# All sums of weight blocks on VectorE: 20 blocks in the first block's output projection, 12 in the third feed-forward

## The chip, the cores and the metric

The kernel runs on one core of one Trainium2 chip, as one program of 53741 instructions in the profile. The time is device microseconds (us) of that core from start to end. Engines are named as in the profile: PE is TensorE (matmuls; PEld its weight loads), DVE is VectorE, ACT is ScalarE, POOL is GpSimd, SP is SyncE, which here only issues DMA transfers.

## The reference

Three transformer-like blocks run one behind the other on a sequence of 1024 tokens of width 1024, all in float32. Cut to what the change touches:

```python
def first_block(x, ...):
    ...
    y = jnp.einsum('bse,ed->bsd', mixed, w_out)      # mixed: 2048 wide, w_out: 2048 x 1024
    ...

def third_block(x, ..., w1, b1, w2, b2, ...):
    ...
    ff = jnp.square(jax.nn.relu(jnp.einsum('btd,df->btf', x, w1[l]) + b1[l]))   # 1024 -> 4096
    ff = jnp.einsum('btf,fd->btd', ff, w2[l]) + b2[l]                           # 4096 -> 1024
    x = layer_norm(DEEPNORM_ALPHA * x + ff, ln2_g[l], ln2_b[l])
```

## The kernel before

**Precision.** A float32 product is made of three products of a faster format: every operand is split into a high part (ACT copies it into the format) and a low part (DVE subtracts the high part from the original), and PE adds high x high, high x low and low x high.

**The third feed-forward** multiplies by a scheme with seven products in place of eight (Strassen-like). It cuts weights in quarters, and four of its seven products take sums of quarters, called S1 to S4, as weights. A *block of sums* is a tile of 128 x 4 x 512 numbers: four quarters q11, q12, q21, q22 come in from the weights in HBM in two transfers of 512 KB, four additions or subtractions of 128 x 512 turn them in place into S4, S3, S1 and S2, and two transfers of 512 KB store them to HBM, from where the feed-forward later loads them like other weights. There are 32 such blocks, 16 for each of the two matrices. The class `WeightSums` (line 1659) does this work: `loads` and `stores` are SP's part, `sums` (line 1699) the arithmetic, each a generator that yields the planned time of its next instruction. Each of the four operations waits for the one before it (semaphore `made`), and the first two also for a transfer (`landed`).

**Where the blocks are made.** `SumsAhead` (line 1725) makes the first 8 blocks and the 16 of the second matrix, 24 in all, far ahead of their use: during the output projection of the first block, in two tiles in turn. The other 8 are made inside the third feed-forward by the object `late` (line 5090), in one tile that lies in a part of y not yet used. In both places the arithmetic is POOL's.

**The output projection** of the first block is `project_chain` (line 307). It has 16 steps, here also called blocks of the projection and counted from 0: two stages of eight output tiles each, of 128 x 1024 results. For each, SP loads 512 KB of weights, ACT makes their high part (line 477), DVE their low part (line 538), PE runs 48 matmuls (lines 429 to 431 for the first two, then 446 to 448), and the result is copied by ACT in the first stage (line 650) or added by DVE in the second (line 655). Two tiles in turn hold the weights, two the results. At its start ACT and DVE also split the inputs: eight tiles mixg, then eight tiles mixa (lines 284 and 291). The loops of PE, ACT and DVE are hardware loops (`Fori`).

**What sets the order.** Each engine has a program of its own, in fixed order, and waits at semaphores. `weave` (line 666) merges generators into one such order by their planned times; the times order instructions on one engine and make nothing wait. The whole phase ends when all engines are through, and SP's program there ends with a wait for all stores of sums (line 372).

**The third feed-forward's engines.** DVE adds products out of the eight banks of results (`combining`, line 5295 by its helper), subtracts what is kept of them (`subtracting`, line 5347, which waits for stores SP issues), makes the low parts of weights (`SevenWeights.low`, line 1816) in seven slots, and those of the inputs. SP's one queue carries raw weights (line 1802), stores of products and differences (lines 5176 and 5183) and the loads and stores of sums (1679, 1686).

## Time and profile before

| | us |
|---|---|
| median of 3 runs | 3939.45 (3936.46 to 3943.36) |
| the profiled execution | 3941.63 |
| its span | 3940.0 |
| PE busy | 3699.2 |
| DVE busy | 2198.1 |
| ACT busy | 1611.7 |
| POOL busy | 822.8 |

The profile is of one execution. Busy time is the sum over an engine's instructions; those of different engines lie beside each other. "Idle before, releaser" is the time an engine stood still ahead of an instruction, and what ended it. TensorE's granted clock is a share of 2.4 GHz. Times in a timeline count from the start of the span.

### The profile page before, as it was taken

Reading aid. Unit: us, or ns where it says so; the run is one execution under the profiler, and the core shown is the slowest. Engines: PE = TensorE matmul, PEld = TensorE weight load, DVE = VectorE, ACT = ScalarE, POOL = GpSimd, SP = SyncE. Lnnn points to the kernel's source line nnn. Section 1 sums busy time; section 2 is a strip of 40 time slices with the busy share of each in tenths; the row PEclk is TensorE's granted clock in tenths of the full one; section 3 lists DMA queues with packets and bytes.
Section 4 is the critical chain, followed back from the end, with each engine's and each line's share of the span. In section 5 each row is a group of like instructions: output and inputs, shape, how many; then the busy total and the mean of one; then the engine's idle time right before and its main releaser. Section 6 shows DMA issues by size and latency. Waiting matters only on the chain. (4 is left out here: it accounts for less than half of the span.)

```text
span 3940.0 us, 53741 instructions
## 1 busy us (share of the span) xinstructions
PE 3699.2 (94%) x20308; PEld 2898.6 (74%) x20308; DVE 2198.1 (56%) x3779; ACT 1611.7 (41%) x2993; POOL 822.8 (21%) x581
## 2 busy tenths in 40 slices
PE   9998999898998887999999989999979988999998
PEld 5787888685766775888888857777667766778876
DVE  3343332415365757766663353666666658667777
ACT  4365222313355514433331154555533326456443
POOL 1000000574002314322210040111433322210012
PEclk9999999998999999999999999999989999999999
DMA  2111111683111112232242021111121105977662
GB/s 88 32 33 47 40 43 43 231 312 123 44 49 49 62 38 97 70 104 94 93 166 86 32 52 55 51 51 49 54 82 50 52 23 180 312 248 249 210 203 95
DMA packets 187744, 393.25 MB, mean 100 GB/s; under 512 B 27992, under 2 KB 34072, under 8 KB 187496
## 3 DMA queue, kind: packets, MB, share of 16 engines
q1 hardware_dynamic: 187496, 389.93, 30.0%
q8 instruction: 157, 2.57, 0.3%
q14 instruction: 91, 0.75, 0.1%
HBM read 293.85 MB, written 97.98 MB: 99 GB/s over the span
## 5 line engine op out<-in xcount | busy, mean ns | idle before, releaser
L1894 PE MATMUL b_ffn_space<-b_ffn_in_hi,b_ffn_wh 128*128 128x512 f32 x896 | 352.1, 393 | 8.2 <-DVE b_ffn_wl L1816 7.2
L1896 PE MATMUL b_ffn_space<-b_ffn_in_hi,b_ffn_wl 128*128 128x512 f32 x896 | 349.9, 390 | 0.0
L1594 PE MATMUL b_ffn_space<-b_ffn_in_hi,b_ffn_wh 128*128 128x512 f32 x728 | 283.9, 390 | 3.3 <-DVE b_ffn_in_x_low L1454 3.3
L1596 PE MATMUL b_ffn_space<-b_ffn_in_hi,b_ffn_wl 128*128 128x512 f32 x728 | 282.8, 389 | 0.0
L1350 ACT ACTIVATE b_ffn_wh<-b_ffn_raw 128x512 fp32r<-128x512 f32 (+1 forms) x152 | 93.6, 619 | 296.8 <-PE b_ffn_space L1622 166.0
L1894 PEld LDWEIGHTS b_ffn_space<-b_ffn_in_hi,b_ffn_wh 128*128 128x128 f32 x896 | 168.7, 188 | 51.7 <-issue 12.9
L1895 PE MATMUL b_ffn_space<-b_ffn_in_x_low,b_ffn_wh 128*128 128x512 f32 x512 | 202.2, 395 | 0.0
L1896 PEld LDWEIGHTS b_ffn_space<-b_ffn_in_hi,b_ffn_wl 128*128 128x128 f32 x896 | 168.7, 188 | 36.4
L1356 DVE TENSOR_TENSOR b_ffn_wl<-b_ffn_raw,b_ffn_wh 128x512 fp32r<-128x512 f32 (+1 forms) x152 | 118.2, 778 | 118.1 <-ACT b_ffn_wh L1350 116.4
L1705 POOL TENSOR_TENSOR b_out_block<-b_out_block 128x512 f32<-128x512 f32 x24 | 37.6, 1565 | 669.6 <-DMA b_out_block<-w 669.6
L1816 DVE TENSOR_TENSOR b_ffn_wl<-b_ffn_raw,b_ffn_wh 128x512 fp32r<-128x512 f32 x224 | 168.5, 753 | 15.1 <-ACT b_ffn_wh L1810 14.3
L762 PE MATMUL na_feed_acc<-b3v_x_hi,na_feed_wh 128*128 128x512 f32 x384 | 164.4, 428 | 2.4 <-DVE na_feed_wl L745 2.4
L1595 PE MATMUL b_ffn_space<-b_ffn_in_x_low,b_ffn_wh 128*128 128x512 f32 x416 | 164.3, 395 | 0.0
L1594 PEld LDWEIGHTS b_ffn_space<-b_ffn_in_hi,b_ffn_wh 128*128 128x128 f32 x728 | 136.3, 187 | 37.3 <-DVE b_ffn_in_x_low L1454 4.1
L1810 ACT ACTIVATE b_ffn_wh<-b_ffn_raw 128x512 fp32r<-128x512 f32 x224 | 133.1, 622 | 64.4 <-PE b_ffn_space L1896 64.3
L1596 PEld LDWEIGHTS b_ffn_space<-b_ffn_in_hi,b_ffn_wl 128*128 128x128 f32 x728 | 136.6, 188 | 28.4
L764 PE MATMUL na_feed_acc<-b3v_x_hi,na_feed_wl 128*128 128x512 f32 x384 | 152.7, 398 | 0.0
L763 PE MATMUL na_feed_acc<-b3v_x_lo,na_feed_wh 128*128 128x512 f32 x384 | 152.6, 397 | 0.0
L1895 PE MATMUL b_ffn_space<-b_ffn_in_own_low,b_ffn_wh 128*128 128x512 f32 x384 | 150.5, 392 | 0.0
L5295 DVE TENSOR_TENSOR b3f_y<-b3f_y,b_ffn_space 128x512 f32<-128x512 f32 x196 | 130.4, 680 | 28.9 <-PE b_ffn_space L1896 28.5
L1620 PE MATMUL b_ffn_space<-b_ffn_in_hi,b_ffn_wh 128*128 128x512 f32 x352 | 136.9, 389 | 0.0
L1622 PE MATMUL b_ffn_space<-b_ffn_in_hi,b_ffn_wl 128*128 128x512 f32 x352 | 136.8, 389 | 0.0
(709 smaller groups left out, 9903.0 us busy)
## 6 DMA issues: line engine op xcount, KB each, us to landing
b_out_block<-w SPq DMA_DIRECT2D x48, 512.0 KB, 5.6
sums_ahead<-b_out_block SPq DMA_DIRECT2D x48, 512.0 KB, 4.1
b_ffn_raw<-w SPq DMA_DIRECT2D x96, 256.0 KB, 4.0
b_ffn_raw<-sums_ahead SPq DMA_DIRECT2D x96, 256.0 KB, 4.6
b_ffn_raw<-w_ffn SPq DMA_DIRECT2D x44, 512.0 KB, 4.6
b_ffn_T<-b3f_y SPq DMA_DIRECT2D x48, 256.0 KB, 4.9
all_x<-b_ffn_T SPq DMA_DIRECT2D x12, 1024.0 KB, 7.3
b_ffn_B<-b3f_y SPq DMA_DIRECT2D x36, 256.0 KB, 4.2
```

Of the source, the lines that this page charges most:

```text
L762: self.nc.tensor.matmul(acc[:], wh[:, wk], xh[:, c], start=(k == 0), stop=False)
L763: self.nc.tensor.matmul(acc[:], wh[:, wk], xl[:, c], start=False, stop=False)
L764: last = self.nc.tensor.matmul(acc[:], wl[:, wk], xh[:, c], start=False, stop=(k == DT - 1))
L1594: self.nc.tensor.matmul(acc, self.weights.wh[w][:, wk], high[:, k], start=(k == 0), stop=False)
L1595: self.nc.tensor.matmul(acc, self.weights.wh[w][:, wk], low[:, k], start=False, stop=False)
L1596: last = self.nc.tensor.matmul(acc, self.weights.wl[w][:, wk], high[:, k], start=False, stop=(k == FAST_ROWS - 1))
L1620: self.nc.tensor.matmul(part, self.weights.wh[w][:, wk], high[:, half], start=(k == 0), stop=False)
L1622: last = self.nc.tensor.matmul(part, self.weights.wl[w][:, wk], high[:, half], start=False, stop=end)
L1816: self.nc.vector.tensor_tensor(self.wl[n % self.slots][:], self.raw[n % self.RAW][:], self.wh[n % self.slots][:], ALU.subtract).then_inc(s ...
L1894: self.nc.tensor.matmul(acc, self.weights.wh[w][:, wk], high[:, k], start=(k == 0), stop=False)
L1895: self.nc.tensor.matmul(acc, self.weights.wh[w][:, wk], low[:, k], start=False, stop=False)
L1896: last = self.nc.tensor.matmul(acc, self.weights.wl[w][:, wk], high[:, k], start=False, stop=(k == FAST_ROWS - 1))
```

## The change

`WeightSums.sums` now takes the engine and its unit as arguments, and yields a planned time for each of its four operations, `each` apart, so that they can be woven among others one by one; SP's planned times follow. In the output projection POOL's program is gone. DVE's hardware loops are replaced by a written-out order, `later()`, that holds the same additions and low parts as before, and is woven with the sums. The plan there begins at 24.0 with a block every 7.2 and operations 0.8 apart (before: 8.0 and 6.7). `SUMS_AHEAD` falls from 8 to 4, so 4 + 16 = 20 blocks are made there and 12 in the feed-forward, where the plan begins at 56.0 with a block every 18.0 (before 70.0 and 16.0) and the sums are woven into DVE's program.

```diff
--- before.py
+++ after.py
@@ -574,6 +574,21 @@
                     low(0, 0, 1, True)
                 done = 2 if ahead is None else 3
                 split_low(nc, ve, split[done:], rounded, split_done, done)
+                if beside is not None:
+                    blocks = [(s, n // 2, n % 2) for s, st in enumerate(stages) for n in range(st.NB)]
+
+                    def later():
+                        yield ASIDE_BLOCK + 4.2
+                        take(*blocks[0])
+                        for g in range(1, len(blocks)):
+                            if g + 1 < len(blocks):
+                                yield ASIDE_BLOCK * g + 5.5
+                                low(*blocks[g + 1])
+                            yield ASIDE_BLOCK * (g + 1) + 4.2
+                            take(*blocks[g])
+
+                    weave(later(), beside.sums(ve, nc.vector))
+                    return
                 take(0, 0, 0)
                 for s, st in enumerate(stages):
                     with ve.Fori(0, st.J - 1) as j:
@@ -603,11 +618,6 @@
                         if n > 1:
                             pool.drain()
                         nc.gpsimd.tensor_tensor(tile[:], (out[:, 0, :] if n == 1 else tile[:]), out[:, n, :], ALU.add)
-
-            if beside is not None:
-                @block.gpsimd
-                def _(pool):
-                    weave(beside.sums(pool))
 
             if join is not None:
                 @block.gpsimd
@@ -1662,8 +1672,9 @@
 
     PLACE = {"S2": 0, "S4": 1, "S3": 2, "S1": 3}
 
-    def __init__(self, nc, ph, name, tiles, sources, out, stored, begin, step):
-        self.nc, self.tiles, self.sources, self.out, self.stored, self.begin, self.step = nc, tiles, sources, out, stored, begin, step
+    def __init__(self, nc, ph, name, tiles, sources, out, stored, begin, step, each):
+        self.nc, self.tiles, self.sources, self.out, self.stored = nc, tiles, sources, out, stored
+        self.begin, self.step, self.each = begin, step, each
         self.landed = [[ph.sem(f"{name}_landed{i}{h}") for h in range(2)] for i in range(len(tiles))]
         self.made = ph.sem(f"{name}_made")
 
@@ -1673,7 +1684,7 @@
     def loads(self, sp, h):
         T = len(self.tiles)
         for n, rows in enumerate(self.sources):
-            yield self.at(n) - 4.5 + 2.6 * (1 - h)
+            yield self.at(n) - 4.5 + 2 * self.each * (1 - h)
             if n >= T:
                 sp.wait_ge(self.stored[n % T][h], 16 * (n // T))
             sp.dma_start(self.tiles[n % T][:, 2 * h:2 * h + 2, :], rows[h].rearrange("p (q s) -> p q s", q=2)).then_inc(self.landed[n % T][h], 16)
@@ -1681,7 +1692,7 @@
     def stores(self, sp, h):
         T = len(self.tiles)
         for n in range(len(self.sources)):
-            yield self.at(n) + 2.9 + 2.6 * (1 - h)
+            yield self.at(n) + 0.3 + 2 * self.each * (2 - h)
             sp.wait_ge(self.made, 4 * n + 2 + 2 * (1 - h))
             sp.dma_start(self.out[n][:, 2 * h:2 * h + 2, :], self.tiles[n % T][:, 2 * h:2 * h + 2, :]).then_inc(self.stored[n % T][h], 16)
 
@@ -1696,22 +1707,24 @@
                 if i < count:
                     engine.wait_ge(sem, 16 * len(range(i, count, T)))
 
-    def sums(self, pool):
+    def sums(self, engine, unit):
+
         T = len(self.tiles)
         for n in range(len(self.sources)):
+            q11, q12, q21, q22 = (self.tiles[n % T][:, q, :] for q in range(4))
             yield self.at(n)
-            q11, q12, q21, q22 = (self.tiles[n % T][:, q, :] for q in range(4))
-            pool.wait_ge(self.landed[n % T][1], 16 * (n // T) + 16)
-            self.nc.gpsimd.tensor_tensor(q22, q21, q22, ALU.add).then_inc(self.made, 1)
-            pool.wait_ge(self.landed[n % T][0], 16 * (n // T) + 16)
-            pool.wait_ge(self.made, 4 * n + 1)
-            self.nc.gpsimd.tensor_tensor(q21, q11, q21, ALU.subtract).then_inc(self.made, 1)
-            pool.wait_ge(self.made, 4 * n + 2)
-            self.nc.gpsimd.tensor_tensor(q11, q22, q11, ALU.subtract).then_inc(self.made, 1)
-            pool.wait_ge(self.made, 4 * n + 3)
-            self.nc.gpsimd.tensor_tensor(q12, q12, q11, ALU.subtract).then_inc(self.made, 1)
-
-
+            engine.wait_ge(self.landed[n % T][1], 16 * (n // T) + 16)
+            unit.tensor_tensor(q22, q21, q22, ALU.add).then_inc(self.made, 1)
+            yield self.at(n) + self.each
+            engine.wait_ge(self.landed[n % T][0], 16 * (n // T) + 16)
+            engine.wait_ge(self.made, 4 * n + 1)
+            unit.tensor_tensor(q21, q11, q21, ALU.subtract).then_inc(self.made, 1)
+            yield self.at(n) + 2 * self.each
+            engine.wait_ge(self.made, 4 * n + 2)
+            unit.tensor_tensor(q11, q22, q11, ALU.subtract).then_inc(self.made, 1)
+            yield self.at(n) + 3 * self.each
+            engine.wait_ge(self.made, 4 * n + 3)
+            unit.tensor_tensor(q12, q12, q11, ALU.subtract).then_inc(self.made, 1)
 
 
 def third_rows(d, s):
@@ -1736,7 +1749,7 @@
 
     def work(self, ph):
         tiles = [ph.sb(f"block{i}", [P, 4, HALF]) for i in range(self.TILES)]
-        return WeightSums(self.nc, ph, "ahead", [t[:] for t in tiles], self.sources, self.out, self.stored, 8.0, 6.7)
+        return WeightSums(self.nc, ph, "ahead", [t[:] for t in tiles], self.sources, self.out, self.stored, 24.0, 7.2, 0.8)
 
     def wait(self, engine):
         for i in range(self.TILES):
@@ -5065,7 +5078,7 @@
                 weave(feed.high(se), feed.taking(se), curving(), exponentials(), placing(), gathered(), norms.squares(se), norms.roots(se))
 
 
-SUMS_AHEAD = 8
+SUMS_AHEAD = 4
 FF3_CHUNKS = D_FF3 // P // DT
 FF3_PAIRS = FF3_CHUNKS * FAST_ROWS
 
@@ -5087,7 +5100,7 @@
 
     with Phase(nc, name) as ph:
         late_stored = [ph.sem(f"late_stored{h}") for h in range(2)]
-        late = WeightSums(nc, ph, "late", [y[:, 0:DT:2, left]], [third_rows(d, s) for s in range(SUMS_AHEAD, PAIRS)], late_sums, [late_stored], 70.0, 16.0)
+        late = WeightSums(nc, ph, "late", [y[:, 0:DT:2, left]], [third_rows(d, s) for s in range(SUMS_AHEAD, PAIRS)], late_sums, [late_stored], 56.0, 18.0, 0.8)
 
         def source(sp, s, o):
             if o not in FAST_SUMS:
@@ -5220,7 +5233,7 @@
                         pool.wait_ge(read_by[o], count)
                         nc.gpsimd.tensor_tensor(quarter(p, q), quarter(p, q), rest[:], ALU.add).then_inc(rest_added, 1)
 
-                weave(norm.pairing(pool), lead.left_sums(pool), late.sums(pool), adding_rests(), all_block_sums())
+                weave(norm.pairing(pool), lead.left_sums(pool), adding_rests(), all_block_sums())
 
             @block.tensor
             def _(pe):
@@ -5399,7 +5412,7 @@
                             done.then_inc(shared_added, 1)
 
                 weave(norm.centring(ve), norm.inverses(ve), norm.scaling(ve), offsetting(), *lead.vector(ve), weights.low(ve), combining(),
-                      *(subtracting(o) for o in places), chunks.lowering(ve), adding())
+                      *(subtracting(o) for o in places), late.sums(ve, nc.vector), chunks.lowering(ve), adding())
 
 
 def third_block(nc, d, consts, cols, x, base, block_sum, carry, sink):
```

**DVE in the output projection, behind the split of the inputs.** `mixa_lo` are low parts of inputs, `out_wl0/1` low parts of weights, `out_block0/1` the two tiles of sums, `ahead` and `out_raw1` the two tiles of raw weights. Before:

```order
L291 TENSOR_TENSOR b1_mixa_lo_5313<-b1_qk,b1_mixa_hi_5312 128x1024 x8
L579 UNCONDITIONAL_BRANCH
L579 ISA
L538 TENSOR_TENSOR b1_out_wl0<-b1_ahead,b1_out_wh0 128x1024
L537 REGISTER_ALU
L538 TENSOR_TENSOR b1_out_wl1<-b1_out_raw1,b1_out_wh1 128x1024
```

Now:

```order
L291 TENSOR_TENSOR b1_mixa_lo_5313<-b1_qk,b1_mixa_hi_5312 128x1024 x8
L538 TENSOR_TENSOR b1_out_wl0<-b1_ahead,b1_out_wh0 128x1024
L1717 TENSOR_TENSOR b1_out_block0<-b1_out_block0 128x512
L1721 TENSOR_TENSOR b1_out_block0<-b1_out_block0 128x512
L1724 TENSOR_TENSOR b1_out_block0<-b1_out_block0 128x512
L1727 TENSOR_TENSOR b1_out_block0<-b1_out_block0 128x512
L538 TENSOR_TENSOR b1_out_wl1<-b1_out_raw1,b1_out_wh1 128x1024
L1717 TENSOR_TENSOR b1_out_block1<-b1_out_block1 128x512
L1721 TENSOR_TENSOR b1_out_block1<-b1_out_block1 128x512
L1724 TENSOR_TENSOR b1_out_block1<-b1_out_block1 128x512
L1727 TENSOR_TENSOR b1_out_block1<-b1_out_block1 128x512
L538 TENSOR_TENSOR b1_out_wl0<-b1_ahead,b1_out_wh0 128x1024
```

The loop is gone; a block of sums stands between the low parts of weight blocks 2, 3 and 4, where one low part stood directly behind the other.

**DVE at the end of the output projection.** `b1y_y` are the results. Before, the last turn of the loop and what follows it:

```order
L655 TENSOR_TENSOR b1y_y<-b1y_y,b1_out_space 128x1024
L537 REGISTER_ALU
L538 TENSOR_TENSOR b1_out_wl1<-b1_out_raw1,b1_out_wh1 128x1024
L655 ISA
L655 TENSOR_TENSOR b1y_y<-b1y_y,b1_out_space 128x1024
L579 REGISTER_ALU
L579 COMPARE_AND_BRANCH
L655 TENSOR_TENSOR b1y_y<-b1y_y,b1_out_space 128x1024
```

Now, from block 18 of the sums on:

```order
L1717 TENSOR_TENSOR b1_out_block0<-b1_out_block0 128x512
L1721 TENSOR_TENSOR b1_out_block0<-b1_out_block0 128x512
L1724 TENSOR_TENSOR b1_out_block0<-b1_out_block0 128x512
L1727 TENSOR_TENSOR b1_out_block0<-b1_out_block0 128x512
L665 TENSOR_TENSOR b1y_y<-b1y_y,b1_out_space 128x1024
L538 TENSOR_TENSOR b1_out_wl1<-b1_out_raw1,b1_out_wh1 128x1024
L1717 TENSOR_TENSOR b1_out_block1<-b1_out_block1 128x512
L1721 TENSOR_TENSOR b1_out_block1<-b1_out_block1 128x512
L1724 TENSOR_TENSOR b1_out_block1<-b1_out_block1 128x512
L1727 TENSOR_TENSOR b1_out_block1<-b1_out_block1 128x512
L665 TENSOR_TENSOR b1y_y<-b1y_y,b1_out_space 128x1024 x2
```

Block 18's four operations and one addition stand ahead of the last low part of weights (of projection block 15), block 19's behind it.

**SP in the output projection.** `L1679` (now `L1690`) loads half a block of sums, `L1686` (now `L1697`) stores half a one, `L368` loads weights of the projection. Before:

```order
L1679 DMA b1_out_block1<-w1_3 128x1024
L1686 DMA sums_ahead<-b1_out_block0 128x1024
L1679 DMA b1_out_block1<-w1_3 128x1024
L1686 DMA sums_ahead<-b1_out_block0 128x1024
L1679 DMA b1_out_block0<-w1_3 128x1024
L1686 DMA sums_ahead<-b1_out_block1 128x1024
L1679 DMA b1_out_block0<-w1_3 128x1024
L1686 DMA sums_ahead<-b1_out_block1 128x1024
L368 DMA b1_ahead<-w_out1a 128x1024
```

Now:

```order
L1697 DMA sums_ahead<-b1_out_block0 128x1024
L1690 DMA b1_out_block1<-w1_3 128x1024
L1697 DMA sums_ahead<-b1_out_block0 128x1024
L1690 DMA b1_out_block1<-w1_3 128x1024
L1697 DMA sums_ahead<-b1_out_block1 128x1024
L1690 DMA b1_out_block0<-w1_3 128x1024
L1697 DMA sums_ahead<-b1_out_block1 128x1024
L1690 DMA b1_out_block0<-w1_3 128x1024
L368 DMA b1_out_raw1<-w_out1a 128x1024
```

Before, the first load of a tile stands ahead of both stores of the other tile; now it stands behind the first of them, and the second load behind the second.

**DVE in the third feed-forward, at the first block of sums.** `ffn_wl` are low parts of weights, `b3f_y<-b3f_y,b3_ffn_space` and `ffn_shared` products added out of the banks. Now (before, the same rows stand there without the four of `L1717` to `L1727`):

```order
L1829 TENSOR_TENSOR b3_ffn_wl2<-b3_ffn_raw0,b3_ffn_wh2 128x512
L5308 TENSOR_TENSOR b3f_y<-b3f_y,b3_ffn_space 128x512
L1829 TENSOR_TENSOR b3_ffn_wl3<-b3_ffn_raw1,b3_ffn_wh3 128x512
L5308 TENSOR_TENSOR b3f_y<-b3f_y,b3_ffn_space 128x512
L1829 TENSOR_TENSOR b3_ffn_wl4<-b3_ffn_raw2,b3_ffn_wh4 128x512
L1717 TENSOR_TENSOR b3f_y<-b3f_y 128x512
L5308 TENSOR_TENSOR b3_ffn_shared3<-b3_ffn_shared0,b3_ffn_space 128x512
L1721 TENSOR_TENSOR b3f_y<-b3f_y 128x512
L1829 TENSOR_TENSOR b3_ffn_wl5<-b3_ffn_raw3,b3_ffn_wh5 128x512
L1724 TENSOR_TENSOR b3f_y<-b3f_y 128x512
L1727 TENSOR_TENSOR b3f_y<-b3f_y 128x512
L5308 TENSOR_TENSOR b3f_y<-b3f_y,b3_ffn_space 128x512
```

The four operations stand among low parts of weights and additions of products, each of which now stands behind whatever they wait for.

## Rows read from the trace of the kernel before

**Rows 1.** The page, part 1: engine busy us, share, instructions.
```profile
PE 3699.2 (94%) x20308; PEld 2898.6 (74%) x20308; DVE 2198.1 (56%) x3779; ACT 1611.7 (41%) x2993; POOL 822.8 (21%) x581
```

**Rows 2.** Stretches of the output projection: busy us per engine, clock, DMA share, GB/s.
```profile
705.00:725.00 20.00, 18.01 (x66) 14.28 (x67) 19.87 (x14) 17.85 (x21) 12.22 (x6) 0.83 0.68 236
725.00:745.00 20.00, 12.63 (x50) 9.87 (x49) 16.63 (x8) 1.97 (x2) 15.09 (x8) 0.83 0.64 217
745.00:865.00 120.00, 120.00 (x523) 97.90 (x522) 20.71 (x15) 16.07 (x16) 86.03 (x63) 1.00 0.89 312
865.00:905.00 40.00, 32.30 (x135) 25.92 (x133) 6.02 (x5) 2.12 (x2) 28.28 (x21) 0.93 0.78 278
```

**Rows 3.** Waits of PE, 700 to 960 us: total, times, longest.
```profile
PE b_out_space L446 <- DVE b_out_wl L538: 9.3, 2, 7.4
```

**Rows 4.** Timeline of DVE, 718 to 770 us: start, us, engine, line, tiles.
```profile
719.34 17.88 DVE L291 TENSOR_TENSOR b_mixa_lo<-b_qk,b_mixa_hi 128x1024 fp32r<-128x1024 f32 x8
737.14 2.28 DVE L538 TENSOR_TENSOR b_out_wl<-b_ahead,b_out_wh 128x1024 fp32r<-128x1024 f32 x1
...
765.72 1.23 DVE L538 TENSOR_TENSOR b_out_wl<-b_out_raw,b_out_wh 128x1024 fp32r<-128x1024 f32 x1 [9.38 <-ACT b_out_wh L477]
```

**Rows 5.** Timeline of ACT, same stretch: results of blocks taken.
```profile
732.25 1.02 ACT L650 ACTIVATE b1y_y<-b_out_space 128x1024 f32 x1 [9.12 <-PE b_out_space L431]
...
752.50 1.03 ACT L650 ACTIVATE b1y_y<-b_out_space 128x1024 f32 x1 [18.29 <-PE b_out_space L448]
...
763.71 1.03 ACT L650 ACTIVATE b1y_y<-b_out_space 128x1024 f32 x1 [9.24 <-PE b_out_space L448]
```

**Rows 6.** Timeline of DVE, 830 to 960 us: results of blocks added.
```profile
862.94 1.22 DVE L655 TENSOR_TENSOR b1y_y<-b1y_y,b_out_space 128x1024 f32 x1 [2.49 <-PE b_out_space L448]
...
899.30 1.22 DVE L655 TENSOR_TENSOR b1y_y<-b1y_y,b_out_space 128x1024 f32<-128x1024 f32 x1 [9.54 <-PE b_out_space L448]
```

**Rows 7.** Timeline of ACT, 830 to 960 us: the stage's end.
```profile
907.29 3.23 ACT L949 ACTIVATE b_head_post_sq<-b1y_y 128x512 f32<-128x512 f32 x6 [21.68 <-PEq L352]
```

**Rows 8.** Timeline of SP's queue, 830 to 960 us: the last stores.
```profile
896.72 7.74 SPq L1686 DMA_DIRECT2D sums_ahead<-b_out_block  x3
```

**Rows 9.** Timeline of POOL, 718 to 770 us: a first sum.
```profile
749.19 1.30 POOL L1705 TENSOR_TENSOR b_out_block<-b_out_block 128x512 f32<-128x512 f32 x1
```

**Rows 10.** Timeline of POOL, 830 to 960 us: the last first sum.
```profile
896.65 1.29 POOL L1705 TENSOR_TENSOR b_out_block<-b_out_block 128x512 f32<-128x512 f32 x1
```

**Rows 11.** Tile b_out_block, 745 to 905 us: ns min/median/max, and landing.
```profile
L1679 SPq DMA_DIRECT2D b_out_block<-w x39: 327/431/774, 746.9 to 894.4; - x39
...
DMA to landing us min/median/max: 2.6/5.1/8.1
```

**Rows 12.** Stretches of the third feed-forward.
```profile
3340.00:3480.00 140.00, 136.02 (x586) 110.51 (x585) 93.34 (x125) 64.16 (x107) 44.76 (x31) 0.99 0.88 299
3480.00:3560.00 80.00, 79.48 (x349) 65.12 (x348) 56.50 (x88) 47.87 (x77) 0.00 (x0) 1.00 0.69 227
```

**Rows 13.** Waits of PE, 3320 to 3540 us.
```profile
PE b_ffn_space L1894 <- DVE b_ffn_wl L1816: 5.3, 5, 2.0
```

**Rows 14.** Waits of DVE, 3320 to 3540 us.
```profile
DVE b_ffn_shared L5347 <- DMA b_ffn_B<-b_ffn_shared: 19.6, 3, 6.7
DVE b3f_y L5347 <- DMA b_ffn_B<-b3f_y: 18.1, 4, 7.2
```

**Rows 15.** Timeline of SP's queue, 3436 to 3484 us.
```profile
3443.15 0.91 SPq L1802 DMA_DIRECT2D b_ffn_raw<-w  x1
3450.64 0.37 SPq L1686 DMA_DIRECT2D b_ffn_sums<-b3f_y  x1
```

**Rows 16.** Timeline of DVE, 3436 to 3484 us.
```profile
3459.24 0.69 DVE L5347 TENSOR_TENSOR b3f_y<-b3f_y 128x512 f32<-128x512 f32 x1 [6.38 <-DMA b_ffn_B<-b3f_y]
```

**Rows 17.** Timeline of PE, 3450 to 3470 us.
```profile
3461.88 0.47 PE L1894 MATMUL b_ffn_space<-b_ffn_in_hi,b_ffn_wh 128*128 128x512 f32 x1 [2.00 <-DVE b_ffn_wl L1816]
```

**Rows 18.** Tile b3f_y, 3330 to 3475 us: landing of its transfers.
```profile
DMA to landing us min/median/max: 2.7/5.6/9.6
```

## The prediction, made before the changed kernel was run

> **What bounds the kernel now.** I read the page's engine line first: PE is busy for 3699.2 us of 3940.0, 94% [rows 1]. An edit that leaves PE's work alone, as this one does, can save only where PE waits, or where a stage ends after PE has finished. So I asked for the busy time by stretch over the two stages that the diff touches, and then for what ended PE's idle time there.
>
> The output projection of the first block runs from about 705 us to 907 us. Its 120 us in the middle have PE busy throughout at a granted clock of 1.00, the 2.4 GHz level. The two stretches ahead of them have 0.83, and 725 to 745 has PE busy for only 12.6 of 20 us. The last 40 us have 32.3 and 0.93 [rows 2]. PE waited there twice for DVE's low weights, 9.3 us in all, 7.4 the longer [rows 3].
>
> The longer wait is at the third block of weights. DVE makes eight low parts of mixa in 17.88 us, 2.24 each, and then the weights' low part in 2.28, from 737.14. With POOL between two sums the same form takes 1.23 [rows 4]. Beside both slow rows POOL was running its sums. ACT takes the results of blocks 1, 2 and 3 (counted from 0) at 732.25, 752.50 and 763.71 [rows 5]: block 2 needs 20.3 us. DVE adds block 12's at 862.94 and block 15's at 899.30 [rows 6]. From block 3 to 12 that is 99.2 us for nine blocks, 11.0 each; at that pace block 15 would have come at 896.0, so 3.3 us more are lost at the end, where the 1.9 us that are left of the 9.3 lie.
>
> The stage doesn't end with its last block: ACT is idle until 907.29 and is held by the start of the next block of the program [rows 7], because SP issues its last stores of sums until 904.5 [rows 8] and waits for them to land. That is 8.0 us from the last result to the next stage.
>
> **Part 1, the projection.** POOL's 96 sums leave and 80 come to DVE. A 128x512 subtraction from SBUF takes DVE 0.69 us [rows 16], so four take 2.8 and all twenty blocks 55 us. DVE was busy for 20.7 of 120 us in the middle [rows 2], so the work itself fits.
>
> The start: with POOL silent I price the eight low parts at 1.23, 9.8 us, and the weights' one at 1.23. From 719.34 [rows 4] that ends at 730.4, before block 1 is finished at 732.25 [rows 5]. So block 2 follows at once and ends at 743.3 instead of 752.50. Where POOL's silence did nothing, the 7.4 us would stay (last rival). What is late next is block 1's own end.
>
> The page "SBUF — State Buffer" of the Trainium skill (section "SBUF: two separate sides") says that a DVE instruction with two SBUF inputs and a POOL instruction that reads SBUF exclude each other for their whole length. By this rule the rows 4 are POOL's doing and the whole 8 x 1.0 us come back; a mere split of bandwidth would agree with the rows as well and gives the same here.
>
> The pace of the sums is the doubtful term, since DVE's order now ties PE to it: a landing that is late holds the low weights queued behind that sum. In SP's new order the two loads of block n+1 stand each behind a store of block n, where they stood one store earlier. So the chain per block is: sums three and four of block n, 1.4 us; a store and a load issued, 0.8, since one issue takes 0.33 to 0.43; landing 5.1, the median of this tile in this traffic [rows 11]; sum two, 0.7. Sum 8.0 us. The same reckoning for before (load behind the first store: 0.8 + 5.1 + 1.3 of POOL) gives 7.2, and the first sums of blocks 4 and 23 stand 147.5 us apart, 7.76 each [rows 9, 10]. I take 8.2, between 8.0 and that plus the 0.56 missed. Bounds: below, the traffic. 312 GB/s at a share of 0.89 [rows 2] is 350 at most; a block moves 2.1 MB and PE takes 0.52 MB of weights in 11.0 us, which leaves 303 GB/s, 6.9 us. Above, 8.8, with landings 0.8 longer. From 2.6 and 8.1, the extremes of [rows 11], it would be 5.5 and 11.0, but every landing would have to be such.
>
> The page "DMA: Bandwidth & Descriptors" of the Trainium skill (its two cost components) has 2.0 us fixed and 436 GB/s: 3.2 us for a half block, which would make the chain 6.1 us and no stall at all. The median of 5.1 here is against it; it is the third rival's reason.
>
> What follows: block 2 ends at 743.3. Behind block 3's result, at 763.71, the next low part starts 2.0 us later [rows 4, 5]; so block 4's is done 3.2 us behind 743.3, at 746.5, and sum 2 stands behind it. Sum 18 then starts at 746.5 + 16 x 8.2 = 877.7, and four sums, one addition (1.22, [rows 6]) and one low part (1.23) later, 5.2 in all, at 882.9, block 15 can start. By PE's own pace it could at 732.25 + 13 x 11.03 = 875.6. So 7.3 us of stall, in small pieces over the last blocks. Without any, block 15 would end at 886.7; with it at 894.0. Then 1.2 for the addition and 1.0, estimated, for the hand-over, since the last sum is made while PE still works: the next stage starts at 896.2 instead of 907.3. **Gain 11.1 us** (18.4 at 7.7 us a block or less, 1.5 at 8.8).
>
> **Part 2, the third feed-forward.** 32 sums leave POOL, 48 come to DVE, and four blocks more are loaded and stored here. PE passes a pair of row blocks, 84 matmuls, in 19.3 us at the later stretch's 349 in 80 us [rows 12]. DVE is busy for 93.3 of 140 us, 67%, where the sums run now and 56.5 of 80 behind them [rows 12], so it has 6.4 us to spare in a pair and 2.8 go to a sum. PE waited 5.3 us in five waits for low weights [rows 13]. The chain behind the longest: SP stands at a store of sums from 3443.15 to 3450.64 [rows 15], so the stores of products behind it come late, DVE waits 6.38 us for one until 3459.24 [rows 16], and PE 2.00 at 3461.88 [rows 17]. DVE's seven waits of that kind are 37.7 us [rows 14]: DVE can stand still for 5 us before PE feels it.
>
> In its place DVE now waits for landings itself. The loads are due 4.5 and 2.9 us ahead of a sum, the second is needed 0.8 into it, and transfers of this tile land in 5.6 at the median, 9.6 at most [rows 18]. So DVE stands for 2 to 4 us at each of 12 blocks, 5 to 7 with the work; bounds per block: 0 where DVE is late anyway, and 5.9 (9.6 less 3.7) by the slowest. SP stands at stores for less long, since DVE's sum is 0.69 instead of 1.3. The first sum falls where DVE has just refilled its lead, and I count 1 us of stall for it; for the others half of the old rate (5.3 us over 8 blocks, so 0.35 each, 4 in all), and the two waits ahead of them stay (their 1.3 is in the 5.3). Together 6.5 for 5.3. **Loss 1.2 us**, bounds a gain of 5.3 and the fourth rival's price.
>
> **Sum.** 11.1 - 1.2 = 9.9 us. The profiled execution took 3941.63 us, of which 3940.0 is the span, and would take 3931.7. It is 2.2 above the median of 3939.45, so the median goes to 3929.5.
>
> **Rivals.** *The sums set the pace.* At 8.8 us a block sum 18 starts at 887.3, block 15 can start 16.9 us late, the gain is 1.5, less 1.2: 3939. For it speaks that loads no longer run ahead; against it, that traffic falls below the present 312 GB/s and landings should shorten.
>
> *Only the tail is won.* If the 2.24 us of [rows 4] aren't POOL's doing, the 7.4 us wait stays, and only the 5.8 us of tail (8.0 less 2.2) come, less 1.2: 3935. The 1.23 of the same form speaks against it.
>
> *No stall anywhere.* Landings shorten to 4.7 or less, the pace to 7.6, and the feed-forward loses its 5.3: 18.4 + 5.3 = 24, so 3916. For it: the total share falls. Against: 5.1 is a median at 0.89.
>
> *Slower: DVE's reserve in the feed-forward is used up.* A sum's 2.8 us and its landing waits of 3.5 are 6.3 of the 6.4 to spare in a pair. From the point where the old waits for stores (37.7 / 7 = 5.4 us) fall into the same pair and don't shrink, DVE is 5.3 us short in it, PE waits as long, and clock is lost beside. Half of the 12 pairs give 32 us: 3939 - 11 + 32 = 3960; half of that is still 3944. For it: the 67% and the long waits in [rows 14]; against it: a late DVE finds its stores and loads landed, and SP's hold, their cause, gets shorter.
>
> **How the numbers follow.** Chances: forecast 0.47, sums set the pace 0.16, tail alone 0.04, no stall 0.18, slower 0.15. About 0.2%, 7.9 us, is what a measurement of this kernel tells from no change. Faster by more: 0.47 less 0.10 for paces above 8.3, and 0.18, so 0.55; within it 0.10 + 0.16 + 0.04 = 0.30; slower 0.15. The range takes in the case without a stall at its lower end, 3916, and the pace of 8.8 with 2 us more lost in the feed-forward at its upper, 3941, and leaves out most of the slower case. The forecast's own is 3923 to 3935.
>
> **What would show it.** Low parts of mixa at 1.23; no PE wait at block 2; POOL idle to 890; first sums of blocks 2 and 18 some 131 us apart; short waits of PE for the low weights in the last five blocks; next stage at about 896 on before's scale; DVE waits of 2 to 4 us for landings of b3f_y, and PE waits near 6.5 us in that stage. It would be wrong if PE waits many times there, or if the sums' pace is outside 7.6 to 8.8.

## The result and the profile after

The changed kernel takes 3953.67 us (median of 20 runs, 3944.99 to 3963.69), the kernel before 3939.4 in the same session (20 runs). The ratio is 1.0037, 95% interval 1.0027 to 1.0047: slower by 14 us. Forecast were 3929.5 and at most 3941. The profiled execution of the changed kernel has a span of 3949.4 us for 3940.0; it ran 2.7 us below the median of its kernel and that of before 2.2 above, so the profiles show 9 of the 14 us.

The stretches of the two stages, after (columns as in [rows 2]):

```profile
705.00:725.00 20.00, 20.00 (x82) 16.01 (x82) 19.86 (x20) 14.60 (x16) 0.00 (x0) 0.94 0.33 116
725.00:745.00 20.00, 20.00 (x88) 16.26 (x87) 8.62 (x12) 3.94 (x4) 0.00 (x0) 1.00 0.72 259
745.00:865.00 120.00, 108.51 (x449) 86.83 (x449) 46.73 (x62) 14.33 (x14) 0.00 (x0) 0.96 0.76 261
865.00:905.00 40.00, 32.24 (x133) 25.53 (x132) 20.34 (x26) 2.12 (x2) 0.00 (x0) 0.96 0.72 246
3340.00:3480.00 140.00, 132.88 (x566) 106.43 (x565) 99.71 (x161) 63.84 (x108) 0.00 (x0) 0.99 0.87 297
3480.00:3560.00 80.00, 78.22 (x341) 63.57 (x341) 58.41 (x93) 41.51 (x73) 0.00 (x0) 1.00 0.91 303
```

Count the matmuls against [rows 2]. In the first 40 us there are 170 for 116: the start came as forecast. In the 120 us in the middle, where before lost nothing, there are 449 for 523. At the 4.36 a microsecond of [rows 2] the 54 are 12 us won (3 of them because the stage began 3.1 us earlier here), and the 74 are 17 us lost.

Waits of PE, 690 to 930 us, after, and then 3325 to 3570 (us in all, times, longest):

```profile
PE b_out_space L446 <- DVE b_out_wl L538: 19.3, 7, 4.4
...
PE b_ffn_space L1907 <- DVE b_ffn_wl L1829: 9.7, 8, 3.5
```

Before had 9.3 in two in the first [rows 3], and 4.5 in four in the second. Waits of DVE in the same two stretches, after:

```profile
DVE b_out_block L1717 <- DMA b_out_block<-w: 64.6, 17, 5.0
DVE b_out_block L1721 <- DMA b_out_block<-w: 28.4, 18, 3.1
...
DVE b3f_y L1717 <- DMA b3f_y<-w: 30.0, 12, 4.9
DVE b3f_y L1721 <- DMA b3f_y<-w: 18.0, 12, 2.9
```

L1717 is a block's first sum, L1721 its second. DVE stood 93 us for their loads in the projection, 48 in the feed-forward.

To tell the stages apart in every profile I use three lengths. The **projection** runs from the end of ACT's last sgu_tmp to the start of ACT's first b_head_post_sq, the **feed-forward** from the start of ACT's first b_ffn_rows of that stage to the start of its first b_ln_sq. Before: 204.9 and 645.9 us. After: 211.7 and 649.5. All else was 3089.2 before and 3088.2 after. Over the profiles below all else lies between 3083.7 and 3097.5 although no edit is meant to touch it, so a single profile places a loss in a stage by the stage's own length, not by the whole span. The rows of ACT that bound the stages, after:

```profile
698.64 0.60 ACT L2480 ACTIVATE sgu_tmp<-sgu_feed_acc 128x512 f32<-128x512 f32 x1 [5.02 <-PE sgu_feed_acc L774]
...
910.96 3.23 ACT L959 ACTIVATE b_head_post_sq<-b1y_y 128x512 f32<-128x512 f32 x6 [23.81 <-PEq L352]
...
3269.94 0.25 ACT L992 ACTIVATE b_ffn_rows<-b_ffn_space 4x128 f32<-4x128 f32 x1
...
3919.45 4.28 ACT L187 ACTIVATE b_ln_sq<-b3f_y 128x512 f32<-128x512 f32 x7 [22.82 <-DVE b3f_y L220]
```

**One block of sums, followed.** SP's queue (SPq in the rows), after; L1697 stores sums, L1690 loads a half block, L368 loads weights:

```profile
809.44 0.33 SPq L1697 DMA_DIRECT2D sums_ahead<-b_out_block  x1
809.81 0.43 SPq L368 DMA_DIRECT2D b_ahead<-w_out1b  x1
810.29 0.72 SPq L1690 DMA_DIRECT2D b_out_block<-w  x1
811.05 0.49 SPq L1697 DMA_DIRECT2D sums_ahead<-b_out_block  x1
811.59 0.43 SPq L1690 DMA_DIRECT2D b_out_block<-w  x1
819.75 0.33 SPq L1697 DMA_DIRECT2D sums_ahead<-b_out_block  x1
```

DVE, after, behind it:

```profile
816.55 0.69 DVE L1717 TENSOR_TENSOR b_out_block<-b_out_block 128x512 f32<-128x512 f32 x1 [4.55 <-DMA b_out_block<-w]
819.02 0.69 DVE L1721 TENSOR_TENSOR b_out_block<-b_out_block 128x512 f32<-128x512 f32 x1 [1.78 <-DMA b_out_block<-w]
...
821.09 1.21 DVE L665 TENSOR_TENSOR b1y_y<-b1y_y,b_out_space 128x1024 f32<-128x1024 f32 x1
825.73 0.69 DVE L1717 TENSOR_TENSOR b_out_block<-b_out_block 128x512 f32<-128x512 f32 x1 [3.43 <-DMA b_out_block<-w]
826.34 1.22 DVE L538 TENSOR_TENSOR b_out_wl<-b_ahead,b_out_wh 128x1024 fp32r<-128x1024 f32 x1
```

PE, after:

```profile
827.61 0.79 PE L446 MATMUL b_out_space<-b_mixa_hi,b_out_wh 128*128 128x512 f32 x1 [4.37 <-DVE b_out_wl L538]
```

Two stores and three loads go out within 2.6 us, and then nothing for 7.7. By about 815 the stores of 809.44 and 811.05 had landed (3.7 us at the median), and their tile was free; but its load stands in SP's program behind a store of the other tile, and that store waits for a sum. The block's second load goes out at 811.59 and is used at 819.02, 7.4 us later. From store to store it is 2.15 + 7.43 + 0.73 = 10.3 us. The other blocks have the same three parts: over the 18 whose second sum waited for its load, the medians are 1.8 us from the first store to the second load, 6.7 from there to the second sum, and 0.7. The next block's first sum stands ahead of the low part of PE's next weights. It comes 3.4 us late, and PE stands still for 4.4, although ACT had made the high part by 816.5.

### The profile page after: what moved, and what is told of

It is laid out like the page before. It is cut to its first block and busy times, and to the rows that moved or that the text cites. A ratio compares the mean times of both kernels' runs of the same rounds, so it can differ in the third digit from the quotient of the medians.

```text
span 3949.4 us, 53722 instructions
## 1 busy us (share of the span) xinstructions
PE 3701.0 (94%) x20308; PEld 2898.5 (73%) x20308; DVE 2245.8 (57%) x3907; ACT 1607.0 (41%) x2993; POOL 634.1 (16%) x453
## 5 line engine op out<-in xcount | busy, mean ns | idle before, releaser
L966 POOL TENSOR_TENSOR b_head_post_sq<-b_head_post_sq 128x512 f32<-128x512 f32 x8 | 10.5, 1329 | 858.0 <-ACT b_head_post_sq L959 858.0
```

## The experiments

Time is the median of each kernel's own runs, ratio against the kernel before on the same chip, with the 95% interval. In the profiles "pace" is the mean distance of the first sums of the projection's blocks. The changed kernel has 9.32 us, before 8.16. The code cuts leave lines out; what a cut doesn't show is said beside it.

**The sums of the projection on another engine.**

```diff
-                    weave(later(), beside.sums(ve, nc.vector))
-                    return
+            if beside is not None:
+                @block.gpsimd
+                def _(pool):
+                    weave(beside.sums(pool, nc.gpsimd))
```

> The changed kernel, but its 20 sums of the output projection run on GpSimd again (four operations a block planned 1.3 us apart), and VectorE runs before's loop of low parts; the third feed-forward keeps its 12 blocks on VectorE. Theory (pace on VectorE): in the changed kernel the projection lost 6.8 us against before because VectorE, which must run in order, waited 93 us for loads of blocks and made the low parts of the weights late. With the sums on another engine, TensorE waits for no low part for more than 1 us, the stage is 11 us shorter than before or more (the sums begin only at 24.0 of the plan, past the two split parts), and the whole stands near 3933 (0.9985 of before), 17 under the changed kernel. Rival 1 (the traffic): the loads and stores of 20 blocks delay the weights whichever engine adds; then the stage stays where it is, near 3950. Rival 2 (GpSimd beside VectorE slows the low parts from 1.23 to 2.3 us): the stage gains some 5 us, near 3945.

Measured: 3924.24 us, 0.9970 (0.9960 to 0.9980). The projection is 184.4 us, 27 shorter than in the changed kernel, with a pace of 8.08; PE waits for no low part of weights. Its middle, in the columns of [rows 2]:

```profile
745.00:865.00 120.00, 120.00 (x525) 98.24 (x524) 24.97 (x17) 16.26 (x16) 87.14 (x64) 1.00 0.89 319
```

The traffic is larger than in the changed kernel (319 GB/s for 261), so it is not what held PE. The time and the stage came out better than the theory, and both rivals fell; the gain of the late start is larger than I had counted: 20.5 us against before. But the run changes more than the engine. With the operations planned 1.3 us apart instead of 0.8, SP's planned times move too, and the first load of a block stands again ahead of both stores of the block before, as in the kernel before. So this run doesn't part the engine from the order; the fourth and the seventh do.

The rows at the start show how GpSimd and VectorE got on there. GpSimd's first sum and VectorE's low parts of mixa:

```profile
710.34 12.23 POOL L1707 TENSOR_TENSOR b_out_block<-b_out_block 128x512 f32<-128x512 f32 x1 [655.62 <-DMA b_out_block<-w]
711.11 9.17 DVE L291 TENSOR_TENSOR b_mixa_lo<-b_qk,b_mixa_hi 128x1024 fp32r<-128x1024 f32 x8
```

The sum's data landed while VectorE was at its low parts. VectorE did all eight at 1.15 us each, and the one sum is listed with 12.23 us, up to 722.57; the next took 1.29. In the kernel before, the two engines were slow side by side, 2.24 and 2.16 an operation. All five runs with the late start on GpSimd have such a row (11.95 to 12.27 us). So the late start, which lets SP load the first block 6 us later in the stage, doesn't keep GpSimd's first sum away from the split parts; but here it was the sum that waited. Why the engines took turns before and not here, no run shows.

**The sums of the feed-forward on another engine.**

```diff
-  *(subtracting(o) for o in places), late.sums(ve, nc.vector), chunks.lowering(ve), adding())
+  *(subtracting(o) for o in places), chunks.lowering(ve), adding())
-  weave(norm.pairing(pool), lead.left_sums(pool), adding_rests(), all_block_sums())
+  weave(norm.pairing(pool), lead.left_sums(pool), late.sums(pool, nc.gpsimd), adding_rests(), all_block_sums())
```

> The changed kernel, but its 12 sums of the third feed-forward run on GpSimd (planned 1.3 us apart), with the 20 of the projection left on VectorE. Theory (two losses): the feed-forward lost about 3.5 to 4 us against before, because VectorE waited 48 us for loads there and TensorE for low weights 9.7 us instead of 4.5; with GpSimd the wait falls to 4 to 6 us and the whole is 4 us under the changed kernel, near 3949 (1.0025 of before). Rival (the feed-forward is the main loss and the landmarks of one execution mislead): near 3942, 10 or more under. Rival (twelve blocks cost what they cost on any engine): no change, near 3953.

Measured: 3952.51, 1.0052 (1.0036 to 1.0067), the changed kernel's time; PE's waits for low weights in the feed-forward are 10.3 us. My theory of a loss through VectorE there fell; "twelve blocks cost what they cost on any engine" stood. (Here too the operations are planned 1.3 us apart, which moves SP's loads and stores with them.)

**Both together:** the split of 20 and 12, all on GpSimd, operations 1.3 us apart.

> The changed kernel's split of blocks (20 and 12) and its plan times, but all sums on GpSimd. Theory: if VectorE is the whole of the loss, this has the gain of the late start without the loss, 10 to 11 us in the projection and nothing lost in the feed-forward: 3929 (0.9973 of before). Rival (four more blocks in the feed-forward cost time on any engine): 3933 to 3936. Rival (traffic in the projection): near 3946.

Measured: 3927.19, 0.9973 (0.9960 to 0.9985). The projection is 184.6, 20 less than before, yet the kernel gains only 11. So the rest is lost elsewhere, and the feed-forward's 12 blocks were the first suspect (649.4 us, PE's waits 9.5), though in this profile they are only 3.5 us of it; all else is 6 longer than in before's profile.

**Only SP's order changed,** VectorE still adding:

```diff
-            yield self.at(n) - 4.5 + 2 * self.each * (1 - h)
+            yield self.at(n) - self.lead + 2 * self.each * (1 - h)     # projection: 7.0
```

> The changed kernel, with the loads of the projection's blocks planned 7.0 us ahead of their sums instead of 4.5, so that both loads of a block stand in SyncE's program ahead of the stores of the block before. Theory (order in the queue): the pace of 9.3 us a block falls to about 7.2 to 7.5, VectorE's waits for loads from 93 us to below 40, TensorE's waits for low weights from 19 us to below 8, and the projection stage becomes 7 us shorter: 3946. Rival (bandwidth or landing time of the loads sets the pace): the pace stays within 0.5 of 9.3 and the time within 3 us of the changed kernel.

Measured: 3937.95, 0.9999 (0.9987 to 1.0011). The pace is 8.24, DVE's waits for loads 59.5 us, PE's for low parts 6.5, the projection 193.0, 19 less than in the changed kernel. The order is most of the cause, 18.7 of the 27.3 us by which the stage was longer than with GpSimd; the bandwidth rival fell. The theory had the direction, but a stage only 7 us shorter and a time of 3946. Its pace of 7.2 to 7.5 was missed because a new wait took over. What SP waited for, 700 to 900 us, in the changed kernel:

```profile
SPq L1697 <- DVE b_out_block L1721: 120.4, 19, 8.0
```

and with the loads ahead:

```profile
SPq L1692 <- DMA sums_ahead<-b_out_block: 103.3, 36, 5.8
```

There (L1692 is the load) a load waits for the tile's last store, which now lands in 6.7 us at the median instead of 3.7: the two tiles set the pace. A third tile wasn't tried.

**The late start alone,** with before's 24 blocks:

```diff
-  self.stored, 8.0, 6.7)
+  self.stored, 24.0, 6.7)
```

> The kernel before, with its 24 sums of the projection on GpSimd planned from 24.0 on instead of 8.0, and nothing else changed. The run with 20 blocks on GpSimd made the projection stage 20 us shorter (184.4 for 204.9), with a pace of 8.0 to 8.1 us a block. Theory (fewer blocks make the room, the late start alone gives nothing): 24 blocks at 8.1 from 727 on end at 921, so the next stage starts near 917 to 922 instead of 907; the split parts are undisturbed, but the time is near 3948 (1.002 to 1.003 of before). Rival (the pace rises when TensorE is never stopped, or the sums overlap the next stage): 3930 to 3935.

Measured: 3939.47, 0.9998 (0.9989 to 1.0007). No stall at block 2, but the end is lost. Waits of PE, 690 to 930 us:

```profile
PE b_head_bank L974 <- POOL b_head_post_sq L956: 28.7, 3, 26.7
```

GpSimd is busy with sums until 904 and only then makes the squares of the next stage. The projection is 206.9. The theory's mechanism was right, its price too high: I had 24 blocks at 8.1 us from 727 on, up to 921. The second block's first sum came at 729.48, and from there on the pace was 7.6 (7.96 with the long first sum), so the sums ended at 904 and the stage is 2 us longer than before's instead of 10 to 15. The time is that of before.

**The count alone,** with the early start: all on GpSimd, 20 and 12 blocks as in the third run, but begin 8.0 and step 6.7 instead of 24.0 and 7.2.

> All sums on GpSimd, 20 in the projection and 12 in the feed-forward, but the projection's planned from 8.0 on with a step of 6.7, as before. Theory (two halves add up): the splits of low parts run beside GpSimd again and TensorE is stopped for some 7 to 9 us at block 2, while the end is free, since 20 blocks at 8.1 end by 873: the stage is about 194 us, and the time near 3934 (0.9985 of before), 7 above the same split with the late start. Rival (the early start costs nothing, only the count matters): the same time as with the late start, 3927.

Measured: 3936.8, 0.9994 (0.9985 to 1.0002). PE waits at block 2 again:

```profile
PE b_out_space L446 <- DVE b_out_wl L538: 10.6, 3, 7.4
```

The projection is 197.9, 4 more than the theory had, and the time 10 above the late start's: the theory holds in the main, the rival falls. The four combinations read: early 24 204.9, late 24 206.9, early 20 197.9, late 20 183.9 to 184.9 (with the step of 7.2). The late start is worth 13 us if the blocks are few enough to end in time, and nothing otherwise.

**VectorE's work without the loads.**

```diff
+            if self.once and n >= T:
+                continue
```

With it, the sums of the later blocks wait for their tile's last stores in place of loads (not in the cut). The kernel adds up stale tiles; it is there for its time alone.

> The changed kernel, but in the projection each of the two block tiles is loaded only once; the 20 sums on VectorE and all 40 stores stay. It leaves out 36 of the 40 loads, so the later sums add up what is left in the tiles. Theory (VectorE's own work of 20 sums costs nothing; it is the waiting for loads that makes the low parts late): VectorE waits for stores only, TensorE waits for low parts less than 5 us, the stage is 186 to 190 us and the time near 3930. Rival (a low part that must wait behind an operation of 1.2 us or a block's chain is late anyway): TensorE's waits stay over 12 us and the time over 3942.

Measured: 3927.59, 0.9969 (0.9958 to 0.9981). The projection is 184.5, the same as with GpSimd; PE waits for no low part of weights. The middle:

```profile
745.00:865.00 120.00, 120.00 (x527) 98.61 (x526) 65.98 (x86) 16.26 (x16) 0.00 (x0) 1.00 0.53 192
```

DVE is busy for 66 of 120 us there, and PE doesn't feel it. The work costs nothing that the stage's length shows. The run also takes away the loads' traffic, but with GpSimd there was more of it than in the changed kernel (319 GB/s for 261) and no loss. So what is left for the projection's loss is VectorE's wait for loads.

**The feed-forward's loads earlier,** the projection's sums on GpSimd:

```diff
+        late.lead = 9.0       # 4.5 before and in the changed kernel
```

> The projection's 20 sums on GpSimd from 24.0 on, the feed-forward's 12 on VectorE with their loads planned 9.0 us ahead of the sums instead of 4.5. Without the last edit it was 3924.2. Theory (VectorE waits 48 us for loads in the feed-forward, and TensorE 6 to 10 us for low weights behind it): TensorE's waits in the stretch from 3325 on fall below 4 us, and the time by 3 to 4 us to 3921. Rival (TensorE's waits there have another cause, since they were 9.5 us with the sums on GpSimd too): no change that can be measured, 3922 to 3927.

Measured: 3910.80, 0.9924 (0.9910 to 0.9937), 13 us under the same kernel without the edit (18 by the ratios of the two) and the fastest of all. The theory's direction held, its size was more than three times too small. The stage is 635.3, 13.9 shorter. The feed-forward, in the columns of [rows 12]:

```profile
3340.00:3480.00 140.00, 140.00 (x616) 115.22 (x615) 111.24 (x176) 74.95 (x120) 0.00 (x0) 1.00 0.96 339
```

616 matmuls for 566 in the changed kernel and 586 before: before, too, PE was losing time here (136.0 of 140 us busy at a granted clock of 0.99). This stage began 15 us earlier than before's; the next run, which begins within 2 us of it, has 615. PE's waits for low weights, 3270 to 3570 us:

```profile
PE b_ffn_space L1899 <- DVE b_ffn_wl L1821: 2.1, 2, 1.3
```

Three more runs put this term in its place. **Both leads, all sums on VectorE** (the changed kernel but for the order of SP):

> The changed kernel with all 32 sums on VectorE and only SyncE's order changed: the projection's loads planned 7.0 us ahead of their sums and the feed-forward's 9.0, instead of 4.5. Measured so far: 3953.7 as changed, 3938.0 with the projection's alone. Theory (the two gains add up, and VectorE itself is no loss): the feed-forward stage falls from 654 to about 641 us, as with the projection's sums on GpSimd, and the time is 3924 to 3927 (0.9965 of before). Rival (the feed-forward's gain needs GpSimd in the projection or was scatter of one chip): 3934 to 3938.

Measured: 3926.85, 0.9958 (0.9944 to 0.9972), as the theory said; projection 195.0, feed-forward 636.1. (The expectation's 654 and 641 count the stage up to ACT's next row, some 4.5 us later; on the scale used here they are 649.5 and 636.5.)

**All on GpSimd, the feed-forward's loads ahead:**

> All 32 sums on GpSimd, 20 in the projection from 24.0 on and 12 in the feed-forward, whose loads are planned 9.0 us ahead instead of 4.5. Measured without the last edit: 3927.2; with the 12 on VectorE and loads ahead: 3910.8. Theory (VectorE's program in the feed-forward waited for loads; GpSimd has nothing behind them): the early loads help GpSimd little, 3924 to 3927. Rival (the early loads help whichever engine adds, since the stores and the slab of y come free sooner): 3911 to 3915.

Measured: 3913.58, 0.9935 (0.9921 to 0.9948); feed-forward 634.8. The theory fell and its rival stood: early loads help GpSimd as much as VectorE. What SP waited for, 3270 to 3570 us, on GpSimd with the short lead (third run) and with the long one:

```profile
SPq L1687 <- POOL b3f_y L1711: 54.9, 12, 6.9
SPq L1689 <- POOL b3f_y L1713: 14.0, 5, 5.7
```

L1687 and L1689 store sums. Behind such a store SP's stores of products and its loads of raw weights stand still. For both stores of every block SP waited 79 us with the short lead and 26 with the long; 44 and 17 with VectorE adding; 56 and 29 with before's eight blocks. That is the link that both engines share. It fits the gain, though no run holds it apart from the loads' own lateness.

**The kernel before with the feed-forward's loads ahead:**

> The kernel before, with the loads of the feed-forward's 8 sums planned 9.0 us ahead instead of 4.5. Theory (its GpSimd has slack: TensorE waited 5.3 us for low weights in that stretch): 0 to 5 us faster, 3934 to 3939. Rival (early loads in this stage are worth 13 us on any engine): 3925.

Measured: 3932.36, 0.9986 (0.9976 to 0.9996); feed-forward 634.7. By the ratio that is 5.5 us (1.6 to 9.5), by the medians 7.3: at or beyond the theory's upper end and short of the rival's 13. With 12 blocks the three pairs of runs have 11 to 14 by the medians and 15 to 18 by the ratios, so with 8 blocks the early loads are worth clearly less.

**A still longer lead in the projection.**

> All 32 sums on VectorE, the projection's loads planned 9.5 us ahead of their sums instead of 7.0 (and 4.5 as changed), the feed-forward's 9.0. With 7.0 the projection stage was 193.0 and 195.0 us in two profiles and the time 3926.9; with the sums on GpSimd the stage was 184 to 185. Theory (what is left of the loss is still loads that come late to a block's first two operations): VectorE's waits for loads fall from 60 us to below 25, TensorE waits for low parts less than 3 us, the stage is 186 to 188, the time 3919. Rival (two tiles and the plan's step set the pace now): the pace stays near 8.2 us a block, the stage at 193 to 195 and the time at 3925 to 3929.

Measured: 3929.71, 0.9965 (0.9952 to 0.9978). The pace is 8.58, the projection 197.4 and DVE's waits for loads 66.6 us, no better than with 7.0 (8.33, 195.0 and 60.2). The theory fell; the rival's direction stands, though pace, stage and time are all slightly worse than it said. SP waited 108.7 us for stores to land before it could load: the tiles set the pace.

## Why the prediction was wrong

Point by point, in its own order.

**PE bounds, and the start.** Right. The eight low parts took 9.17 us in all, the weights' one 1.22, and ACT took the results of blocks 1 to 3 at 728.04, 739.12 and 750.22, 11.1 apart; no wait at block 2. From the timeline of DVE, after:

```profile
712.89 9.17 DVE L291 TENSOR_TENSOR b_mixa_lo<-b_qk,b_mixa_hi 128x1024 fp32r<-128x1024 f32 x8
721.97 1.22 DVE L538 TENSOR_TENSOR b_out_wl<-b_ahead,b_out_wh 128x1024 fp32r<-128x1024 f32 x1
```

**The pace of the sums: the step that failed.** Forecast 8.2 us, measured 9.32, beyond the bound of 8.8. The term that failed is the landing. From a block's first store to the next block's second load I had 2.2 us (sums three and four 1.4, issue 0.8); measured are 1.8 at the median, and 2.15 in the block followed above. From there to the second sum I had 5.1; measured are 6.7 at the median, and 7.43 in that block. The last sum has its 0.7. The 5.1 was a median over loads and stores mixed [rows 11]. The page has them apart; after:

```profile
b_out_block<-w SPq DMA_DIRECT2D x40, 512.0 KB, 6.1
sums_ahead<-b_out_block SPq DMA_DIRECT2D x40, 512.0 KB, 3.7
```

Before, the same two lines say 5.6 and 4.1. With 5.6 the chain would have been 8.5, so a third of the miss stood in before's page; the rest is new. And the landing isn't a constant of the traffic: it rose to 6.1 although the traffic fell from 312 to 261 GB/s, against what I argued under the first rival. VectorE makes a block's four sums in 2.9 us, so its stores and the next loads go out nearly together. GpSimd needs 5.4, and with its late start and 20 blocks loads landed in 5.2 to 5.5. With the loads ahead of the stores (fourth experiment) it is the loads that are quick, 4.9, and the stores that are slow, 6.7: in these two runs, what is issued first in a burst lands sooner. So I read the burst as the cause, though no run isolates it. The Trainium skill's page "DMA: Bandwidth & Descriptors" (its two cost components) has a fixed part of 2.0 us and 436 GB/s, fitted, as it says, on another issuing path than SP's; the estimate from it is 3.2 us for such a transfer. This case's rows don't agree while other transfers are in flight: the medians in the projection are 3.7 to 7.2, and only with the loads left out did the stores land in 2.8.

With the pace at 8.24, as in the fourth experiment, the projection was 11.9 us shorter than before. The forecast was 11.1 at 8.2. At 8.33 and 8.58, the two later runs with early loads, the working gives 9.0 and 5.0, and the stage was 9.9 and 7.5 shorter. So the working from pace to stage is good to some 2 us, and the term put into it was wrong. At 9.32 the working has sum 18 at 746.5 + 16 x 9.32 = 895.6 and block 15 able to start 5.2 later, 25.2 behind PE's own pace instead of 7.3. Of the 18.4 us without a stall that leaves a loss of 6.8, what the profiles show (211.7 less 204.9). That the two agree to a tenth is luck: PE's waits for low weights were 19.3 us, not 25.2, and they lay elsewhere.

**The place of the stall.** Wrong. I had it in the last blocks, but PE's seven waits run from 798 to 898. I let the sums run at their own pace and compared only the end; in an engine that runs in order each late load holds whatever stands behind it, here from block 8 on.

**The tail.** Right: from the start of the last addition to the next stage it was 1.6 us (909.34 to 910.96) for 2.2 forecast, where before had 8.0.

**The feed-forward: the second term that failed.** Forecast a loss of 1.2 us; the two profiles have 3.6 (649.5 less 645.9). The stage lengths, for 12 blocks with the short lead (seven profiles), are 646.2 to 653.2, mean 649.1. For 8 blocks there are only two, 645.9 and 640.3. With the long lead all five are 634.7 to 636.1. So by the means late loads cost 14 us with 12 blocks and about 8 with 8, and the change lost some 6, whichever engine adds; with two profiles 5.6 us apart on one side, that is known to within a few us only. I priced PE's waits that carried a name, and for the four blocks more only their VectorE time, by half of the old rate; that the loads' lateness cost time in the stage already before, I put at nothing. Of the whole 14 us, 6.8 in the projection and about 6 here are 13.

**The rivals.** "The sums set the pace" named the mechanism, but its own bound of 8.8 stopped 0.5 short. "DVE's reserve is used up" had the sign right and the mechanism wrong: GpSimd in VectorE's place won nothing in the feed-forward, and with all sums on VectorE and the loads ahead, DVE is busy for 113 of 140 us and PE never waits for it. Its rows with both leads:

```profile
3340.00:3480.00 140.00, 140.00 (x615) 114.93 (x614) 112.84 (x180) 77.49 (x126) 0.00 (x0) 1.00 0.96 341
```

What stays open: why the same feed-forward varied by 7 us between profiles and by 1.4 once the loads came early, by which path the late loads reached PE there, and why the burst lands late.

## What to carry to other kernels

Before work is moved onto an engine that feeds the critical one, ask not how busy that engine is but what it will wait for, and what is queued behind each wait. The same 20 sums cost nothing on VectorE when no load was waited for, and 27 us of a stage when loads came late. Find the loop of load, compute and store in the issuing queue's program: a load behind a store of the block before can't run ahead into the second buffer, and putting it ahead was worth 15 us here. Take landing times for loads and stores apart, from the rows of the traffic in which they will run.

## What was not expected of the hardware

Loads of 512 KB landed in 6.1 us at the median (one in 7.4) at 261 GB/s, and in 5.2 at 319. The order and spacing of the issues went with it, the DMA share did not (0.76 and 0.89). In the feed-forward PE worked for 140 us without idle time beside 339 GB/s of traffic, at a DMA share of 0.96. A sum of GpSimd that met VectorE's row of eight low parts was listed with 12.23 us for 1.29, and VectorE lost nothing. And a wait can cost more than its length: in the projection's middle PE was idle for 11.5 of 120 us, its granted clock was 0.96 for 1.00, and it made 74 matmuls fewer, 17 us' worth. Behind the 4.37 us wait shown above, matmuls started every 0.43 us, before it every 0.23.
